# Half-wide decay products, subtractions on GpSimd and new places for dense groups in a two-block transformer kernel

## The reference, cut to what matters

```python
y = rms_norm(x) @ w_in + b_in          # split into mq mk mv mo mi mf | hq hf hi hg | sq sk sv
# mLSTM, 4 heads of 64: causal conv and silu on mq, mk; gates mi, mf; output gate sigmoid(mo)
# HGRN2, 4 heads of 64: query silu(hq), per-channel decay from hf, values hi, output gate silu(hg)
log_f = logaddexp(log(lb), log1p(-lb) + log_sigmoid(hf));  key = (1 - lb) * sigmoid(-hf)
A[l, s] = sum_d q[l, d] * exp(G[l, d] - G[s, d]) * key[s, d]   for s <= l,  G = cumsum(log_f)
# sliding-window attention, 8 query heads, 2 key heads, window 128, rotary, sinks
x = x + concat(m_out, h_out, s_out) @ w_out
x = x + square(relu(rms_norm(x) @ w_up)) @ w_down;  x = x + sigmoid(...) * e
```

## Time and profile before

| what | value |
|---|---|
| median of 3 runs | 3160.41 us (3159.9 to 3169.08) |
| the profiled execution | 3157.43 us, span of its trace 3155.6 us |
| PE busy | 2879.8 us, 91% of the span |
| DVE / ACT / POOL busy | 1667.7 / 1106.7 / 108.0 us |
| mean granted TensorE clock | 0.951 |
| DMA | 280.86 MB, mean 89 GB/s |

### The profile page before, as it was taken

How to read it: one execution, slowest core, us unless ns; L and a number is a source line. 1 busy time by engine, 2 the same in 40 slices (tenths; PEclk the granted TensorE clock), 3 DMA queues, 4 the chain that set the end, 5 groups by cost and what they waited for, 6 DMA issues and landing times. The chain is left out here.

```text
span 3155.6 us, 37966 instructions
## 1 busy us (share of the span) xinstructions
PE 2879.8 (91%) x14756; PEld 2346.2 (74%) x14756; DVE 1667.7 (53%) x3011; ACT 1106.7 (35%) x1691; POOL 108.0 (3%) x88
## 2 busy tenths in 40 slices
PE   4798999999787989999996998899998998999998
PEld 3676778887666867888875887788886786778886
DVE  3656575555657555656655544553444544454442
ACT  4334332223453343222243444332332344332231
POOL 1000000000200000000020000000000000000000
PEclk9988899999888978999998999999998999999999
DMA  3110144443121102444422210132322210122322
GB/s 133 64 44 27 47 143 158 160 160 140 60 81 45 54 27 75 166 160 173 153 80 95 81 40 28 54 107 75 110 77 94 81 53 19 64 81 82 112 77 77
DMA packets 42993, 280.86 MB, mean 89 GB/s; under 512 B 5944, under 2 KB 6200, under 8 KB 11704
## 3 DMA queue, kind: packets, MB, share of 16 engines
q1 hardware_dynamic: 42808, 278.34, 25.4%
HBM read 276.23 MB, written 2.10 MB: 88 GB/s over the span
## 5 line engine op out<-in xcount | busy, mean ns | idle before, releaser
L303 DVE TENSOR_TENSOR low_panels<-raw_panels,high_panels 128x2048 fp32r<-128x2048 f32 (+3 forms) x218 | 469.2, 2153 | 345.1 <-ACT high_panels L291 345.0
L291 ACT ACTIVATE high_panels<-raw_panels 128x2048 fp32r<-128x2048 f32 (+3 forms) x218 | 392.5, 1801 | 494.9 <-PE bank L1419 150.6
L420 PE MATMUL bank<-mlp_h_high,high_panels 128*128 128x512 f32 x1152 | 457.3, 397 | 0.0
L420 PE MATMUL bank<-mlp_h_low,high_panels 128*128 128x512 f32 x1152 | 455.2, 395 | 0.0
L420 PE MATMUL bank<-mlp_h_high,low_panels 128*128 128x512 f32 x1152 | 455.1, 395 | 0.0
L420 PEld LDWEIGHTS bank<-mlp_h_high,low_panels 128*128 128x128 f32 x1152 | 216.1, 188 | 52.6
L420 PEld LDWEIGHTS bank<-mlp_h_low,high_panels 128*128 128x128 f32 x1152 | 216.2, 188 | 51.5
L420 PEld LDWEIGHTS bank<-mlp_h_high,high_panels 128*128 128x128 f32 x1152 | 216.2, 188 | 51.5
L445 PE MATMUL bank<-high_panels,h_high 128*128 128x256 f32 x704 | 211.6, 301 | 13.3 <-DVE arena L1100 12.7
L420 PE MATMUL bank<-h_high,high_panels 128*128 128x512 f32 x496 | 207.7, 419 | 12.9 <-DVE arena L1080 12.8
L1419 PE MATMUL bank<-mlp_hid_high,high_panels 128*128 128x512 f32 x512 | 204.5, 399 | 0.0
(11 more groups left out here) (344 smaller groups left out, 4900.5 us busy)
## 6 DMA issues: line engine op xcount, KB each, us to landing
raw_panels<-in_w SPq DMA_DIRECT2D x238, 1024.0 KB, 4.9
raw_panels<-in_w SPq DMA_DIRECT2D x16, 384.0 KB, 3.2
raw_panels<-in_w SPq DMA_DIRECT2D x4, 960.0 KB, 4.6
raw_panels<-in_w SPq DMA_DIRECT2D x4, 768.0 KB, 4.2
row<-in_row SPq DMA_DIRECT2D x2, 1220.0 KB
x<-in_xT SPq DMA_DIRECT2D x1, 2048.0 KB, 7.6
raw_panels<-in_w SPq DMA_DIRECT2D x4, 512.0 KB, 3.5
mix<-in_rope SPq DMA_DIRECT2D x2, 1024.0 KB, 7.7
```

What stands on the lines that cost most here:

```text
L291: self.nc.scalar.activation(self.g.high[:, i % SPLIT, 0:raw.shape[1]], raw, ACT.Copy).then_inc(self.high_ready, 1)
L303: self.nc.vector.tensor_tensor(self.g.low[:, i % SPLIT, 0:w], raw, self.g.high[:, i % SPLIT, 0:w].bitcast(F32), ALU.subtract).then_inc(sel ...
L420: ins = nc.tensor.matmul(bank[:, :], w[a][:, k, c0:c0 + P], rhs[b][:, k0 + k, :], start=first and k == 0 and j == 0, stop=last and k == kt ...
```

## The change

- **Opening.** The two opening stages become one. x is loaded in two halves ahead of everything else. The bounds of both layers are computed there once, and a layer only copies its own.
- **Levels.** In levels 1 to 7 of a half the products take only the query blocks that are later in their pair: 64 instead of 128 columns. `keep` masks 256 instead of 512 columns in levels 1 to 5. Levels 6 and 7 are copied by ACT, block by block. The two subtractions of `prepare` move to GpSimd. ACT takes its exponential two levels ahead, DVE its multiplications one ahead.
- **Banks.** Groups 0 to 7 each get a bank of their own.
- **Dense groups.** The order of panels becomes mv, mo, sk/sv, sq, sq, hg. Groups 8 to 20 (now with mo) stand between levels, `hg` (4 groups) between pairs 0 to 3, and only the 12 groups of the window heads stay between the mLSTM blocks, all by block 8. The rotation moves one block earlier. The first output groups stand one pair later, and the chunks' order changes.
- The sigmoid of mo moves from pair 0 to level 17, the silu of hg from pair 0 to pair 4.

The core of the diff (the new line numbers are shifted; all that is left out repeats these edits on the other engines or renames):

```diff
...
+MASKED = 5
...
-    out += [k("w_in", c) for c in (C_MVO, C_SKV, C_SQ, C_SQ + PW, C_MVO + PW, C_HIG + PW)]
+    out += [k("w_in", c) for c in (C_MVO, C_MVO + PW, C_SKV, C_SQ, C_SQ + PW, C_HIG + PW)]
...
+                sp.dma_start(g.x[:, 0:DC // 2, :], a["xT"][:, 0:DC // 2, :]).then_inc(s("x_begun"), 16)
+                sp.dma_start(g.x[:, DC // 2:DC, :], a["xT"][:, DC // 2:DC, :]).then_inc(s("x_loaded"), 16)
+                sp.dma_start(kc[:, :], a["kc"]).then_inc(s("start_loaded"), 16)
+                sp.dma_start(g.cond[:, :], a["cT"]).then_inc(s("start_loaded"), 16)
+                sp.dma_start(pos[:, :], a["pos"]).then_inc(s("tables_loaded"), 16)
...
                 sp.dma_start(k1[:, :], a["k1"]).then_inc(s("tables_loaded"), 16)
-                sp.dma_start(pos[:, :], a["pos"]).then_inc(s("tables_loaded"), 16)
                 pan.load_first(sp, 0, s("first_panel_loaded"))
...
+                dve.wait_ge(s("bound_log"), 1)
...
+                act.wait_ge(s("x_begun"), 16)
+                for c in range(DC):
+                    if c == DC // 2:
+                        act.wait_ge(s("x_loaded"), 16)
+                    square_chunk(nc, act, g, e, c, g.x[:, c, :])
+                act.wait_ge(s("start_loaded"), 32)
+                nc.scalar.activation(g.cond[:, :], g.cond[:, :], ACT.Silu)
+                act.wait_ge(s("bound_abs"), 1)
+                sa.link(nc.scalar.activation(parts[:, 3, :], parts[:, 3, :], ACT.Exp, scale=-1.0))
+                nc.scalar.activation(parts[:, 3, :], parts[:, 3, :], ACT.Ln, bias=1.0).then_inc(s("bound_log"), 1)
+                act.wait_ge(s("rope_steps"), 2 + NT + 16)
+                nc.scalar.activation(cs[:, :, :, :].rearrange("p a t r -> p (a t r)"), small[:, 128:192], ACT.Sin)
...
+                for i in range(DEPTH):
+                    nc.scalar.activation(bounds[:, i, 3, :], bounds[:, i, 2, :], ACT.Exp)
 
...
         n_before = 8
-        window_groups = list(range(at_panel[7], at_panel[10]))
+        window_groups = list(range(at_panel[8], at_panel[11]))
+        hg_groups = list(range(at_panel[11], at_panel[12]))
...
-        dense_h = {1: [8], 3: [9], 5: [10], 7: [11], 9: [12], 11: [13], 13: [14], 15: [15], 17: [16]}
+        dense_h = {2 * i: [n_before + i] for i in range(5)}
+        dense_h.update({10 + i: [n_before + 5 + i] for i in range(8)})
         dense_m = {}
-        for i, j in enumerate(range(17, 37)):
-            dense_m.setdefault(2 * i // 3 if i < 12 else i - 4, []).append(j)
-        dense_w = {i: [first_groups[c]] for c, i in enumerate((7, 8, 9, 10, 12, 13, 16, 17))}
-        chunk_w = {2: [2], 3: [3], 5: [0], 6: [1], 7: [4], 11: [5], 15: [6], 18: [7]}
+        for i, j in enumerate(window_groups):
+            dense_m.setdefault(3 * i // 4, []).append(j)
+        dense_w = {i: [hg_groups[i]] for i in range(NT)}
+        dense_w.update({i: [first_groups[c]] for c, i in enumerate((8, 9, 10, 12, 13, 14, 16, 17))})
+        chunk_w = {4: [0], 5: [1], 6: [2], 7: [3], 8: [4], 11: [5], 15: [6], 18: [7]}
         chunk_order = [c for i in sorted(chunk_w) for c in chunk_w[i]]
...
         def dense_bank(i):
-            return bank[1 + i % 2]
+            return bank[(3, 4, 1, 2, 5, 6, 0, 7)[i]] if i < n_before else bank[1 + i % 2]
 
         def released(eng, i):
-            if i < 0:
+            if i < n_before:
+                i = {n_before: 2, n_before + 1: 3}.get(i + 2)
+            if i is None:
...
+                pool.wait_ge(s("g_summed"), 2)
...
+                    nc.gpsimd.tensor_tensor(out[:, :, B:2 * B], blk[:, :, B:2 * B], ref, ALU.subtract).then_inc(s("d_span"), 1)
+
+                for k in range(n_levels):
+                    prepare(k)
                 add_squares(nc, pool, g, nx)
...
                     released(pe, i - 2)
+                    if i == hg_groups[0]:
+                        pe.wait_ge(s("w_turned_kept"), 6)
...
+                    if k == 1:
+                        pe.wait_ge(kept_v, by_dve[n_before])
                     if lv > 0:
...
                     for i, (sx, t0, t1) in enumerate(todo):
-                        n = (t1 - t0) * P
+                        within = 0 < lv <= TILE_LEVELS
...
                             kk = hx[r, 2 + c, sx * P:(sx + 1) * P] if lv == 0 else W[r, slot, sx * P:(sx + 1) * P]
-                            ins = nc.tensor.matmul(level_bank(k, m)[:, o:o + n], kk, q, start=True, stop=True)
+                            to = level_bank(k, m)[:, o:o + n]
+                            if within:
+                                B = LEVELS[lv - 1]
+                                q = q.rearrange("p (b w) -> p b w", w=2 * B)[:, :, B:2 * B]
...
                         dense(i)
-                    products(k)
                     if k == NL + 1:
                         results(0)
-                    if k == 18:
+                    products(k)
+                    if k == 15:
                         turn_gates()
+                    if k == 17:
+                        spread(0)
                 for j in range(n_blocks):
                     hd, kt = blocks[j]
-                    if j == 2:
+                    if j == 1:
                         results(1)
-                    if kt == 0:
-                        spread(hd)
+                    if kt == 2 and hd + 1 < MH:
+                        spread(hd + 1)
                     for i in dense_m.get(j, []):
                         dense(i)
                     block_scores(j)
                     if kt == 2 and hd >= 1:
                         block_result(hd - 1)
-                for c in range(6):
+                    if j == n_blocks - 2:
+                        turn_window(0)
+                        turn_window(1)
+                turn_window(2)
+                block_result(MH - 1)
+                for c in range(3, 6):
                     turn_window(c)
-                    if c == 1:
...
+                    if lv <= MASKED:
                         return
...
+                        if lv == MASKED + 1 and m == 0:
+                            level_kept(act, NL * c + MASKED)
+                            if c == 1:
+                                act.wait_ge(s("d_out"), 1)
                         b = level_bank(k, m)
-                        if lv == TILE_LEVELS + 1:
+                        if lv <= TILE_LEVELS:
+                            B = LEVELS[lv - 1]
+                            for o in range(0, P, 2 * B):
+                                ins = nc.scalar.activation(AT[o:o + B, m, :].rearrange("p (t w) -> p t w", t=NT)[:, :, o + B:o + 2 * B],
+                                                           b[o:o + B, 0:2 * P].rearrange("p (t w) -> p t w", t=NT)[:, :, o // 2:o // 2 + B], ACT.Copy)
+                        elif lv == TILE_LEVELS + 1:
                             ins = nc.scalar.activation(AO[:, m, 0:6:5, :], b[:, 0:2 * P].rearrange("p (b w) -> p b w", b=2), ACT.Copy)
...
+                    if k + 2 < n_levels:
+                        decay(k + 2)
...
-                    if k == 11:
+                    if k == 10:
                         gate_logs()
-                    if k == 13:
+                    if k == 17:
                         conv_open()
+                        act.wait_ge(kept_v, by_dve[at_panel[8]])
+                        nc.scalar.activation(mo, mo, ACT.Sigmoid).then_inc(s("mo_open"), 1)
+                        act.wait_ge(s("gates_by_token"), 1)
+                        nc.scalar.activation(em, cm[:, 16:32], ACT.Exp, scale=-1.0).then_inc(s("em_ready"), 1)
+                block_exp(0)
                 keep_apart(n_levels - 1)
                 squares = Steps(s("w_squares"))
-                act.wait_ge(s("gates_by_token"), 1)
-                nc.scalar.activation(em, cm[:, 16:32], ACT.Exp, scale=-1.0).then_inc(s("em_ready"), 1)
                 behind = []
+
+                def keep_window(c):
+                    act.wait_ge(s("w_turned"), c + 1)
+                    nc.scalar.activation(qsT[:, c, :], bank[c % 3][:, :], ACT.Copy).then_inc(s("w_turned_kept"), 1)
...
@@ -1029,23 +1122,22 @@
                     if j == 9:
                         act.wait_ge(squares.sem, squares.n)
                         nc.scalar.activation(ss, ss, ACT.Sqrt, bias=g.eps, scale=1.0 / HD).then_inc(s("w_root"), 1)
-                        act.wait_ge(s("head_squares"), 1)
-                        nc.scalar.activation(hs[:, 0:16], hs[:, 0:16], ACT.Sqrt, bias=g.eps, scale=1.0 / HD).then_inc(s("head_root"), 1)
-                for c in range(6):
-                    act.wait_ge(s("w_turned"), c + 1)
-                    nc.scalar.activation(qsT[:, c, :], bank[(0, 7)[c % 2]][:, :], ACT.Copy).then_inc(s("w_turned_kept"), 1)
+                    if j == n_blocks - 2:
+                        keep_window(0)
+                        keep_window(1)
+                for c in range(2, 6):
+                    keep_window(c)
...
```

(52 more changed lines are left out.)

214 lines of the change are left out of this document (98 added, 116 removed).

## The result

The changed kernel takes 3120.97 us (median of 4 runs, 3119.96 to 3125.75) against 3161.48 (4 runs, 3159.90 to 3169.08): the ratio is 0.9875, interval 0.9855 to 0.9895. Forecast were 3078 us and a range from 3045 to 3120. The sign was right; of 82 us of gain about 40 came, and the median lies just outside the range. The profiled execution took 3119.96 us, its span is 3118.2.

What follows compares the result with a forecast made beforehand. PE with its stops was taken to bound the front, levels' first half and blocks, DVE the second half, an engine-to-engine chain the pairs. Two layers at 36.5 us plus the opening gain 82: 3078 us, range 3045 to 3120.

Steps and rivals of the forecast that it cites:

- Opening: Start of the kernel, once: x in halves lets the squares begin earlier; gain 9 us (5 to 12).
- Front: Start of each layer: PE's two stops fall away, 22.4 us at full clock instead of 39.4; gain 17.0 us.
- Levels, first half: First half of the levels, per layer: half-wide products at 0.85 us a level; 37 us against 44.7, gain 7.5.
- Pool: Subtractions in the levels: 0.7 us each on Pool; its holds charge DVE 4 us in the second half, none in the first.
- Levels, second half: Second half of the levels, per layer: PE 38, DVE 37, 7 us of waits, 4 for Pool; 50 us, 2.5 lost.
- Blocks: mLSTM blocks, per layer: 50 us to block 8, then DVE leads; 78 us against 100.8, gain 22.5 (15 to 27).
- Pairs: Pairs, per layer: four hg groups come in, so the second output groups begin 8 us later (0 to 15).
- Pool's holds in full: Rival, levels: DVE pays all of Pool's holds, 9 to 23 us a layer; 3108 us; 20 in 100.
- The clock stays low: Rival: DVE-led blocks 9 to 15 leave 1.2 GHz for hg groups and pairs, 9 to 10 us a layer; 3097; 13 in 100.
- Seams better than my walk: Rival: no loss in the pairs, nothing for Pool, 12 us a layer; 3054 us; 12 in 100.
- Pool sets the pace: Rival, levels: waits for Pool's two subtractions, at 4 us an instruction 63 us a layer lost; 3204 us; 4 in 100.
- little is gained: Rival: the log-decay chain holds the front and DVE the blocks, 35 us a layer of waits; 3155 us; 3 in 100.

Runs made afterwards that it cites:

- order two: The changed kernel with DVE making a panel's low part behind the eviction of its token group, not ahead of it: 3102.79 us, 0.9813 of the kernel before.

## Why the prediction was half right

- **Opening**, 9 us: 10.1 (36.06 to 25.96 us at the first norm spread). Right.
- **Front**, 17.0 us: 59.9 to 48.6 us, and 5.6 for group 8 that is now in it: 16.9. Right; layer two gained 15.3.
- **Levels, first half**, 37 us from group 8 on: 38.1. The mis-sized term is the half-wide product, 0.85 us a level taken, 1.11 measured for 16 instructions, as good as the full-wide 1.16. The upper end of my own bound was the answer. The row of the results, 64 columns too, gave 0.117 us; I halved it on the thought that two could lie beside each other, and no row showed that.
- **Pool**, 0.7 us an instruction: 0.61 alone, 0.74 and 0.84 as means, up to 1.58. 4 us of holds: 4.4 on the multiplications. The price was right; the place was not, since 2.7 of the 4.4 lay in the first half, where I had charged nothing, and only 1.7 in the second. The rule of the Trainium skill that I had weighed (GPSIMD Engine Reference, Performance pitfalls for Q7 kernels), half more for steps above 8 bytes, showed in no level; but these views step by 4 bytes inside a block, and by 8 in level 1, so no run here puts it to the test.
- **Levels, second half**, 50 us: 54.9. I charged 7 us for two waits; they were 4.1 and 6.1, and each was followed by matmuls at 1.2 GHz, for which I had charged nothing. My sum was off as well: 38 + 7 + 4 is 49, and DVE's 38.3 less 12.4 and more 6.8 is 33, not 37.
- **Blocks**, 78 us: 94.7. This is the step that failed, by 16.7 us a layer; the other misses, 1.1 and 4.9 in the levels and 4.0 the other way in the pairs, leave 2.0. "Twelve groups (33.6) and what belongs to blocks 0 to 8 (16) take 50 us": it was 63.4. The groups took 40, 6.4 us more than I had: some 4.5 of them the clock (one group took 4.6 and one 5.4 us, two together 6.4, the others 2.9 to 3.0 each), the rest that a group between small products takes 2.9 to 3.0 us and not 2.8. Stops took 5.2 (1.3, 3.1, 0.8), and the remaining 18.2 were the rest of PE's work, where I had 16. The tail, 28, was 31.3, at a clock of 0.56. In words: I took PE as busy without a break, as DVE had room there (busy for 50.2 of 100.8 us), and did not walk the order on DVE. An engine with little to do still makes another wait when what it does first is the wrong thing. That the stop of 3.1 us is such a case is shown by order two, 18.6 us; why the clock was low where no stop stood ahead stays open.
- **Pairs**, -8 us: -4.0. They cost half as much as I thought; which of the three terms was too dear no run shows.
- **Sum**: 36.5 a layer, 18.1 and 17.8 measured; block two gave 6 us back that stood in no term.
- **Rivals.** Pool's holds in full: no; with the subtractions on DVE the levels took 4 us a layer more. The clock stays low, 3097: its mechanism was there, but in the second half of the levels, between the dense groups and in the blocks' tail, where I had looked for it in the pairs alone; 13 in 100 was too little for it. Seams better than my walk: only in the pairs. Pool sets the pace, and little is gained: no.

## What to carry to other kernels

Where an engine has room, its order still needs a walk: for every buffer that the leading engine waits for, ask what stands ahead of the release on the idle engine; two lines moved behind an eviction brought 18.6 us. Price a stop of TensorE with the slow matmuls behind it (here 5.2 us of stops and 4.5 of clock in blocks 0 to 8), and judge a kernel whose clock is in motion by several runs: the profiles of two kernels whose runs can't be told apart stood 16 us apart. Before you compare two stretches, let both begin and end at the same instruction. Narrower matmuls paid nothing here, 64 for 128 columns, with a weight load of 63 ns beside each.

## What the runs showed of the hardware

- The granted clock fell at stops (0.51 from 141 to 146 us, behind one of 4.1 us), and also where there was hardly one: 0.50 from 163.0 to 173.2 us with PE busy all the time, and for 23.1 of the 25 us from 160 to 185. Runs of one program spread over 19 us with it.
- Matmuls without a reader raised the clock of the blocks' tail from 0.57 to 1.00, and five fills of 2.85 us did not lengthen it (31.4 us without, 30.6 with). Two of them right ahead of the turns shortened it from 30.9 to 27.1 and 26.3 us.
- At the turn of block two's loop DVE sat idle for 0.70 to 5.79 us ahead of one small instruction, 4.37 and 5.79 in two executions of one program, 5.20 and 2.71 of another. By the code it waits there for three small loads. The Trainium skill (Runtime: NRT & Kernel Launch, Instruction fetch mechanics) has a taken branch break the sequential prefetch; no run here shows that this, or that the loads, are the cause.
